# A two-direction chunked scan on TensorE: the backward direction's transposes, Gram products and state products write the opposite half of the partitions, so that they can be issued in fours with the forward direction's

## The reference

```python
def wkv_scan(s0, r, decay, k, v, kk, b, reverse, emit):
    xs = tuple(jnp.moveaxis(t, 1, 0) for t in (r, decay, k, v, kk, b))

    def step(s, inp):
        r_t, w_t, k_t, v_t, kk_t, b_t = inp
        sa = jnp.einsum('bhij,bhj->bhi', s, kk_t)
        s = s * w_t[:, :, None, :] - sa[..., None] * b_t[:, :, None, :] + v_t[..., None] * k_t[:, :, None, :]
        y = jnp.einsum('bhij,bhj->bhi', s, r_t) if emit else None
        return s, y

    s_final, ys = lax.scan(step, s0, xs, reverse=reverse)
```

## Time and profile before

| | |
|---|---|
| times of three executions | 4361.62, 4368.76, 4371.81 us (median 4368.76) |
| span of the profiled execution | 4373.1 us |
| scan stage, first sums to last output | from 1805.3 to about 2392 us of the span |
| TensorE busy over the whole span | 4006.2 us (92%) |

### The profile page before, as it was taken

The page is one execution under the profiler, slowest core; times in us unless marked ns, Lnnn a source line. Parts: engine busy times, 40 slices in busy tenths (PEclk is TensorE's granted clock), DMA queues, the critical chain, the costliest instruction groups (busy, mean ns, idle before and its releaser), DMA issues. The chain is left out here.

```text
span 4373.1 us, 83873 instructions
## 1 busy us (share of the span) xinstructions
PE 4006.2 (92%) x35140; PEld 3268.1 (75%) x35140; DVE 1793.8 (41%) x3271; ACT 1455.5 (33%) x3118; POOL 687.3 (16%) x549
## 2 busy tenths in 40 slices
PE   8999899998999996699998899988978899999998
PEld 2789888776889993589998344467975677888886
DVE  3323344555532117545554644754124362111234
ACT  2111177555521115433332500043124652212133
POOL 0000064100100491233332700010000000000001
PEclk9999999999999997799999799999988999999999
DMA  8223453102423476522222502152242231111121
GB/s 345 74 94 119 116 98 82 34 19 78 168 75 98 152 242 225 172 49 69 70 63 54 188 21 82 39 198 82 87 150 84 80 121 49 49 50 50 34 91 72
DMA packets 291297, 439.84 MB, mean 101 GB/s; under 512 B 76980, under 2 KB 210708, under 8 KB 286399
## 3 DMA queue, kind: packets, MB, share of 16 engines
q1 hardware_dynamic: 290664, 429.81, 31.0%
q10 hardware_dynamic: 288, 5.07, 0.3%
HBM read 315.76 MB, written 124.03 MB: 101 GB/s over the span
## 5 line engine op out<-in xcount | busy, mean ns | idle before, releaser
L416 PE MATMUL g_acc<-g_wh,l_x_high 128*128 128x320 f32 (+5 forms) x1824 | 590.0, 323 | 12.2 <-DVE g_o L464 6.8
L416 PE MATMUL g_acc<-g_wh,l_x_low 128*128 128x320 f32 (+5 forms) x1824 | 588.7, 323 | 0.0
L416 PE MATMUL g_acc<-g_wl,l_x_high 128*128 128x320 f32 (+5 forms) x1824 | 588.7, 323 | 0.0
L416 PEld LDWEIGHTS g_acc<-g_wh,l_x_high 128*128 128x128 f32 x1824 | 345.4, 189 | 18.9 <-DVE g_o L464 7.1
L416 PEld LDWEIGHTS g_acc<-g_wl,l_x_high 128*128 128x128 f32 x1824 | 345.6, 189 | 2.8
L416 PEld LDWEIGHTS g_acc<-g_wh,l_x_low 128*128 128x128 f32 x1824 | 345.2, 189 | 2.3
L440 ACT COPY g_o<-g_acc 128x320 f32<-128x320 f32 (+6 forms) x120 | 54.5, 454 | 768.3 <-PE g_acc L416 744.6
L464 DVE COPY g_o<-g_acc 128x320 f32<-128x320 f32 (+6 forms) x120 | 62.6, 524 | 576.2 <-PE g_acc L416 543.9
L3223 PE MATMUL ffi_acc<-l4a_x_high,ffi_wh 128*128 128x512 f32 x704 | 274.0, 389 | 0.9 <-DVE ffi_wl L54 0.9
L3223 PE MATMUL ffi_acc<-l4a_x_high,ffi_wl 128*128 128x512 f32 x704 | 273.9, 389 | 0.0
L3223 PE MATMUL ffi_acc<-l4a_x_low,ffi_wh 128*128 128x512 f32 x704 | 273.9, 389 | 0.0
(11 more groups left out here) (537 smaller groups left out, 9275.5 us busy)
## 6 DMA issues: line engine op xcount, KB each, us to landing
scan_F<-s_FE SPq DMA_DIRECT2D x160, 192.0 KB, 3.9
s_FE<-feat_f SPq DMA_DIRECT2D x10, 2304.0 KB, 7.8
l4a_first_w<-in_w_ffn_in SPq DMA_DIRECT2D x44, 512.0 KB, 3.8
g_cu<-s_U SPq DMA_DIRECT2D x24, 768.0 KB, 5.4
pj_o<-s_O SPq DMA_DIRECT2D x26, 512.0 KB, 4.5
front_w<-in_attn_ada_w SPq DMA_DIRECT2D x8, 1536.0 KB, 11.1
front_w<-in_rec_ada_w SPq DMA_DIRECT2D x8, 1536.0 KB, 13.0
g_wr<-in_w_ffn_out SPq DMA_DIRECT2D x44, 256.0 KB, 2.7
```

The source lines that it names most:

```text
L416: mm = pe.matmul(acc[r][:, 0:it["n"]], left, right, start=(k == 0 and q == 0), stop=(k == kt - 1 and q == 2))
```

## The change

The backward direction's transposes, Gram products and products that make or read the state read half i and write half 1-i (`HALF[i ^ d]`). Its `KB`, `AR`, `S` and the totals for `eT` thus lie in swapped halves, while `GA`, `GB`, the values and all of the doubling lie as before: a swap on the way in and one on the way out cancel. No elementwise instruction changes, and the number of products stays the same. The new helper `corners` issues the two forward products (diagonal quadrants) and the two backward ones (the other two quadrants) behind one another. Used are fours in `turn`, `grams`, `mix_s`, and in a new `from_state` (the products with the state, taken out of `mix_w` and `mix_y`).

The order on TensorE becomes: `mix_w`, `turn(n, 1)` (`qk` of both directions), `mix_u`, `turn(n, 2)` (`qa` of both), `mix_s`, `grams(n, 1, 2)` and `grams(n, 0, 0)` for both directions, k = 0, `begin_y` (the state's products for `y`, both directions), forward `mix_y`, k = 1, and so on. Every four waits for both directions. `totals` (the products over one column) go ahead of `step` k = 2 and 4. The backward products that add onto what another quadrant has put in the same place of PSUM wait for a semaphore, `from_state` or `totals`.

```diff
+                def corners(of, c0, n, left, right, start=True, stop=True):
+                    for d in range(2):
+                        for i in range(2):
+                            mm = pe.matmul(bank[d][of][HALF[i ^ d], c0:c0 + n], left(d)[HALF[i], :], right(d)[HALF[i], :], start=start, stop=stop)
+                        if d == 0:
+                            first = mm
+                    return first, mm
+
+                def totals(n, d):
+                    s, b, f = e[d], bank[d], F[d][n % 3]
                     pe.wait_ge(s[f"loaded{n % 3}_"], 64 * (n // 3 + 1))
                     if n:
                         pe.wait_ge(s["g_out"], n)
+                    for h in range(NP2):
+                        for i in range(2):
+                            mm = pe.matmul(b[0][HALF[i ^ d], 256 + h:257 + h], f[HALF[i], 3, h, :], one[HALF[i], :], start=True, stop=True)
+                    mm.then_inc(s["totals"], 1)
+
+                def sums(n, d):
+                    s, b, f = e[d], bank[d], F[d][n % 3]
+                    pe.wait_ge(s["totals"], n + 1)
                     for hb in HALF:
-                        pe.matmul(b[0][hb, 0:256], tri[hb, 2 * d, hb], flat(f[hb, 3, :, :]), start=True, stop=True)
-                    for h in range(NP2):
-                        mm = pairs(b[0], 256 + h, 1, f[:, 3, h, :], one[:, :])
+                        mm = pe.matmul(b[0][hb, 0:256], tri[hb, 2 * d, hb], flat(f[hb, 3, :, :]), start=True, stop=True)
                     mm.then_inc(s["sums"], 1)
...
+                def turn(n, to):
+                    of = [qk[d][n % 2] if to == 1 else qa[d] for d in range(2)]
+                    for d in range(2):
+                        pe.wait_ge(e[d]["scaled"], 4 * n + 2 * to)
...
+                    for x in range(2):
                         for h in range(NP2):
+                            for d in range(2):
+                                for i in range(2):
+                                    mm = pe.matmul(bank[d][to][HALF[i ^ d], x * 256 + h * C:x * 256 + (h + 1) * C], of[d][HALF[i], x, h, :], ident[HALF[i], HALF[i]], start=True, stop=True)
+                                if x and h == NP2 - 1:
+                                    mm.then_inc(e[d]["turned"], 1)
+
+                def grams(n, x, to):
+                    for d in range(2):
+                        pe.wait_ge(e[d]["a_out"], n + 1)
+                        pe.wait_ge(e[d]["kb_out"], n + 1)
+                        pe.wait_ge(e[d]["exps"], 4 * n + 4)
+                    for h in range(NP2):
+                        done = corners(to, h * P, P, lambda d: KB[d][:, x, h, :], lambda d: AR[d][n % 2][:, h, :, :].rearrange("p x t -> p (x t)"))
+                    for d in range(2):
+                        done[d].then_inc(e[d]["grams"], 1)
...
+                def from_state(n, x):
+                    for h in range(NP2):
+                        done = corners(3, h * C, C, lambda d: AR[d][n % 2][:, h, x, :], lambda d: S[d][n % 2][:, h, :], h == 0, False)
+                    done[1].then_inc(e[1]["from_state"], 1)
+
+                def stated(n, x):
+                    pe.wait_ge(e[1]["from_state"], n + 1 + x + max(n - CCH, 0))
...
+                    from_state(n, 0)
+                    for d in range(2):
+                        if d:
+                            stated(n, 0)
                         for h in range(NP2):
-                            pairs(b[3], h * C, C, AR[d][n % 2][:, h, 0, :], S[d][n % 2][:, h, :], True, False)
-                            mm = pairs(b[3], h * C, C, GK[d][n % 2][:, h, 0, :], F[d][n % 3][:, 1, h, :], False, True)
-                        mm.then_inc(s["w_mm"], 1)
+                            mm = pairs(bank[d][3], h * C, C, GK[d][n % 2][:, h, 0, :], F[d][n % 3][:, 1, h, :], False, h == NP2 - 1)
+                        mm.then_inc(e[d]["w_mm"], 1)
...
+                        pe.wait_ge(e[d]["u_out"], n + 1)
+                    for h in range(NP2):
+                        corners(3, 256 + h * C, C, lambda d: qk[d][n % 2][:, 0, h, :], lambda d: F[d][n % 3][:, 1, h, :], True, False)
+                        done = corners(3, 256 + h * C, C, lambda d: qk[d][n % 2][:, 1, h, :], lambda d: Un[d][:, h, :], False, True)
+                    for d in range(2):
+                        done[d].then_inc(e[d]["s_mm"], 1)
+
+                def begin_y(n):
+                    for d in range(2):
+                        pe.wait_ge(e[d]["s_out"], n + 1)
+                        pe.wait_ge(e[d]["gr"], n + 1)
+                    from_state(n, 1)
...
                     if n < NCH:
-                        turn(n, 0)
+                        turn(n, 1)
                     if n:
                         mix_u(n - 1)
                     if n < NCH:
-                        turn(n, 1)
-                        grams(n, 0)
+                        turn(n, 2)
                     if n:
                         mix_s(n - 1)
                     if n < NCH:
-                        grams(n, 1)
+                        grams(n, 1, 2)
+                        grams(n, 0, 0)
                     for k in range(8):
+                        if n + 1 < NCH and k in (2, 4):
+                            totals(n + 1, k // 2 - 1)
                         if n < NCH and k < 2:
                             step(n, 1, (k,))
                         elif n < NCH:
                             step(n, k)
+                        if n and emits(n - 1) and k == 0:
+                            begin_y(n - 1)
```

More of the change, by code:

```diff
@@ L1553, in turn @@
                         if n:
                             if to == 1:
[L1555 removed]
+                                pe.wait_ge(e[d]["power"], 5 * n)
                             else:
[L1557 to L1561 removed]
@@ L1655, in _ @@
                 pe.wait_ge(cleared, 5)
-                for d in range(2):
-                    sums(0, d)
+                totals(0, 1)
+                totals(0, 0)
+                sums(0, 0)
+                sums(0, 1)
                 for n in range(NCH + 1):
```

39 lines of the change are left out of this document (6 added, 33 removed).

## The result

The changed kernel takes 4415.14 us (median of 4 runs, 4409.91 to 4417.93), the kernel before in the same measurement 4368.52 (4361.62 to 4371.81). The ratio is 1.0107, with an interval of 1.0092 to 1.0121: 46.6 us slower, where 20 us faster was forecast. All times are those of the fast executions; one of e10_spread_filled took 6517.87 us, at a clock of 0.553 where its others had 0.95, and is left out. The profiled execution has a span of 4414.0 us, 40.9 more than that of the earlier trace rows.

The account below looks back on a forecast made before the run. TensorE's queue bounds the scan at 28.80 us a chunk. Saved 65 us, plus 45 for clock falls, 2 in the first chunk, less 3.4 for the old fall: -21, -20 with fours at 0.12; 4368.8 - 20 = 4349 us, range 4333 to 4362 (overall 4300 to 4375).

Parts of the forecast that it names:

- About 0.45 of this is stalls ended by nothing that the profile shows, which I keep: TensorE in a scan chunk: of 2.0 us idle in 28.8, some 0.45 is unexplained stalls, carried over unchanged.
- 14 x 25.45 + 11 x 3.0: Chunks with output: 25.45 us each at full clock, plus 11 falls of the clock losing 3.0 us each.
- Fours at 0.12 us: Four 64-column products in four quadrants cost 0.12 us, about a pair's price; all fours save 5.5 us a chunk with output.
- Rival 2: Quadrants take turns: a 64-column four costs 0.233 us, waits and clock falls stay; 33 us slower, 4402; chance 0.15.
- the prediction's own signs of being wrong: A four over 0.13 us, PEclk in the scan staying near 1.00, or a wait appearing behind k = 2.
- Rival 3: Issue binds in part: 9 ns an instruction, a four at 0.144 us, 12 us on top, 4361; chance 0.08.
- (c): Ahead of k = 0: TensorE waits for POOL's mid because only x = 0 Gram products cover the chain; 2.33 us idle.
- (d): Ahead of begin_y: TensorE waits for both directions' states, 0.89 us idle; without output, k = 1 waits 1.7 instead.
- (e): From k = 2 on: steps find their operands because totals fill the former waits; no idle counted.
- (a): Start of mix_w: from_state waits for both directions' y_out, 0.15 us idle.
- (b): From from_state through mix_s: ACT's AR of both directions is ready at 5.65 us, TensorE done at 5.3; 0.35 us idle.
- The clock: New idle stretches halve TensorE's clock for 6.8 us in three of four chunks with output, all others; 45 us lost.

Follow-up runs that it names:

- e10_spread_filled: e6 with idle products of 256 columns where TensorE waits (ahead of the Gram products, begin_y and the inverse's first step): 4374.1 us, ratio 1.0007.
- e3: Changed kernel with three wait-free streams of products (pairs, fours of 64 columns, fours of 128) ahead of the scan's loop; run once for its trace, not timed.
- e7: Changed kernel with 42 idle products of 64 columns ahead of the inverse's first step, making a chunk 1792 instructions, 7 times 256: 4418.4 us.
- e8: e7 with 64 more idle products (128 instructions) ahead of the scan's loop, which itself stays the same: 4405.4 us.
- e9: Changed kernel with 20 idle products of 256 columns in diagonal pairs ahead of the inverse's first step, in place of e7's fillers: 4399.3 us.
- e1: Changed kernel's order and waits, but backward products back in the same halves as the forward ones, so a four is two pairs in turn: 4430.6 us.
- e6: Changed kernel reordered: mix_s between the Gram stages, begin_y and forward mix_y ahead of the inverse's first step, VectorE making state before both starts: 4385.1 us.
- e13: e6 with the backward products back in the same halves as the forward ones, so it has no fours: 4411.5 us.
- e2: Changed kernel's order with only the Gram products in fours; turns and state products go one direction after the other: 4414.2 us.
- e5: Changed kernel with both turns ahead of mix_u, then ordered as e6, and only the Gram products in fours: 4383.7 us.
- e14: e6 with only the Gram products in fours, and idle products of 256 columns in the chunks without output alone: 4377.7 us, ratio 1.0020.

## Why the prediction was wrong

**The step that failed** is the term "About 0.45 of this is stalls ended by nothing that the profile shows, which I keep". What the runs show in its place is that TensorE gets its instructions in pieces of 256, at best one in some 3.47 us (e3), and stops at the end of a piece when it uses them faster or the next one comes late (e7, e8). I kept the stops at their size before and did not ask what makes them; they were the one sign in the old profile of the limit that the change then ran into. In the trace before they lie at the same multiples of 256 instructions. In the changed kernel they measured 3.25 us a chunk instead of 0.45: 14 x 2.8 = 39 us in the chunks with output. Against the forecast's 14 x 25.45 + 11 x 3.0 = 389.3 us the 14 chunks took 436.0, 46.7 more. The stops are 39.2 of it, the work +9.2 (27.5 a chunk before the change where I had 26.8), the waits +4.4 (4.0 against 3.7), and -6 is left for the falls of the clock and the fours. The +9.2 was in the prediction's own rows: it found 2.0 us idle in a chunk of 28.8, named 0.45 of stalls and 1 us of waits, and dropped the rest. The four chunks without output hold 12.4 us of stops, where they held 2.9. Outside the 14 chunks the forecast missed another 21 us: some 9 in the four without output, 5 in the first, 7 in the last two.

**Fours at 0.12 us: right** where they run, 15 ns a product. Rival 2 (the quadrants take turns) had the right side, 4402, for the wrong reason. None of the prediction's own signs of being wrong came (a four over 0.13 us, PEclk near 1.00, a wait behind k = 2), so nothing in it tested the term that failed. The words "what no row shows is the rate of issue" named the place, but I bounded the rate within a single four, 0.117 to 0.233 us, and not over hundreds of instructions. Rival 3 had 9 ns an instruction as its price; sustained it is 13.6. The Trainium skill's two rules cited ahead of the result ("TensorE: Matmul & The Clock Gate", What overlaps and what doesn't, and "Wait — 56ns, not 53.3ns?") would give 29 ns (two pairs in turn) and 25 ns from product to product. The trace disagrees inside a piece (15 ns); over a long stream it comes out at 27 ns (3.47 us for 128), by the supply of instructions.

**The waits (c), (d) and (e): right.** The idle time ahead of k = 0 was forecast at 2.33 and stands as 2.10 idle after the last product's own end; ahead of `begin_y` 0.89 was forecast and 1.26 measured by the profile's rows; nothing new stands behind k = 2 (DVE's transpose, 5.3 us before, 4.8 after). (a) and (b) were half a microsecond in sum; the wait for `AR` appears (5.9 us, 10 times), but stops stand in the same place and mix with it.

**The clock: right in its sum, by luck in part.** In the 14 chunks 64.9 us passed at half clock, against 11 x 6.83 = 75. But they are 16 falls, 13 of them of 3.41 us and not 6.83: more and shorter ones, and the two errors cancel. PEclk was 0.93; my 0.85 did not even follow from my sum, which makes 1 - 37.6 / 389 = 0.90. The first chunk lost more than the 2 us forecast: it spent 17 us more at half clock than before. e9 confirms the price.

**The total.** The new order costs 62 us (e1 against before), fours everywhere give back 15 where I counted some 100. In e6's order they give back 26.4 (e13 against e6). What else they saved went into stops (2.2 us a chunk in either order), waits and falls of the clock.

**What stays open.** The round of 3.47 us explains the smaller part of the stops in the kernel. Had each transfer started 0.25 us after the boundary or 3.47 us after the one before it, whichever is later, some 16 of the changed kernel's 45.5 us would be left, and none of e1's 14.2. The other transfers start late. In e7 the piece that `qa` waits for starts 1.8 to 2.7 us after the boundary before it and 4.2 to 5.4 us after the transfer before it, in each of the 14 chunks, always around `mix_w`. This makes stops of 1.6 to 2.8 us, where in the three chunks shown the round alone would make 0.6 to 0.8. It would also explain why the Gram products alone in fours (e2, e5, e14) still have 1.7 to 2.0 us of stops a chunk.

What the traces show there is SyncE's data transfers, the stores of `Yo` and the loads of `scan_F`. Windows of e7 from the boundary to the start of the piece that `qa` waits for, in those three chunks, and last the same for another piece (columns as in the earlier trace rows):

```profile
2080.45:2082.74 2.29, 2.29 (x126) 2.29 (x124) 1.52 (x4) 0.74 (x2) 0.00 (x0) 1.00 0.99 236
2111.55:2113.90 2.35, 2.35 (x129) 2.35 (x127) 1.57 (x4) 0.74 (x2) 0.00 (x0) 1.00 0.98 232
2143.09:2145.78 2.69, 2.67 (x133) 2.53 (x129) 1.92 (x5) 0.74 (x2) 0.00 (x0) 1.00 1.00 226
...
2139.59:2140.52 0.93, 0.93 (x38) 0.93 (x36) 0.42 (x1) 0.43 (x3) 0.00 (x0) 1.00 0.00 0
```

The DMA share is 0.98 to 1.00 where the piece is late and 0.00 where it is not. Over the changed kernel's 14 chunks, 40.0 of the 45.5 us of stops follow pieces for which data transfers took over 20% of the DMA engines between the boundary and the start of the instruction transfer; so do all 6.4 us in the kernel before, all 14.2 in e1, and 34.6 of 41.8 in e7. Of the changed kernel's pieces without a stop only 11 of 58 are such. With the first stops of e3 this makes the data transfers the first suspect. It is not shown as the cause: no run moved them, 5.5 us of the changed kernel's stops have few or none before them, and once (the transfer at 2228.63) an instruction transfer started 5.4 us after its boundary although no data moved.

## What to carry to other kernels

Before making an engine's instructions shorter, divide its time a stage by its instruction count: where 256 instructions of TensorE take less than about 3.5 us (e3), the rest of the saving turns into stops. So products of 128 columns can gain from four quadrants (13.6 ns an instruction in e3), and those of 64 columns hardly. Look also at what data transfers are in flight when a new piece of instructions falls due. Stalls that the profile puts down to "issue" are to be located before they are carried into a sum: look whether they lie at equal distances in instructions, as they did already in the trace before. And interleaving two directions for the sake of the array makes each chain wait for both, which here cost four times what the fours gave.

## What was not expected of the hardware

- TensorE's instructions come in pieces of 256 (16 KB on the queue "q8 instruction"). In e3's stream one came every 3.47 us, and it was usable 2.3 us after the transfer's start: 13.6 ns an instruction.
- Where data transfers fill the DMA engines (share 1.04), a piece's transfer started up to 5.97 us after the boundary (e3), against 0.2 to 0.3 us at a share of 0.02.
- In four quadrants products of 64 columns start every 15 ns (32 in 0.69 us), with their weight loads beside them. Each product lasts 0.22 us, so these loads go to row groups that a product of the other column group is using, and do not wait for it.
- A product of 64 columns with weights of the whole array took 113 ns in a row of 42 (e7), about four times that of a pair's.
